# A sibling's front and first refills, and another order of the last expert weights, in a block with a mixture of 32 experts

## Reference

```python
h = rms_norm(x, norm1_gain);  proj = h @ w_in               # columns: q,k,v | q_i (512), k_i (64), w_i (8) | retention
out_a = dsa_attention(...)    # each query attends to its 64 best keys by an indexer score
out_b = silu(g_b) * retention(...)
x = x + concat(out_a, out_b) @ w_out
h2 = rms_norm(x, norm2_gain)
logits = h2 @ w_router + b_router;  top 4 of 32, softmax over the four -> combine
for e in range(32):
    z = h2 @ w1[e] + b1[e]                                  # w1[e]: 1024 x 2048, 8 MiB
    act = clamped_swiglu(z)
    out += combine[:, e] * (act @ w2[e] + b2[e])            # w2[e]: 1024 x 1024, 4 MiB
x = rms_norm(x + out, final_gain)
```

## Time and profile before

| | |
|---|---|
| median of 3 runs | 1087.22 us (1087.14 to 1087.7) |
| the profiled execution | 1086.36 us |
| its span, first to last instruction | 1084.6 us |
| PE busy, share of the span | 1038.4 us, 96% |
| DVE, ACT, POOL busy | 302.7, 157.0, 22.2 us |
| DMA, mean over the span | 396 GB/s, 429.75 MB |
| mean granted clock of TensorE | 0.985 of 2.4 GHz |

### The profile page before, as it was taken

One profiled execution on the slowest core, in us unless ns is written; L12 is line 12 of the kernel. 1 busy time (PEld: TensorE's weight loads), 2 busy tenths in 40 slices (PEclk: granted clock), 3 DMA queues, 4 the chain that ended last, 5 costly groups with the idle time before them and its releaser, 6 DMA issues.

```text
span 1084.6 us, 11586 instructions
## 1 busy us (share of the span) xinstructions
PE 1038.4 (96%) x4616; PEld 397.4 (37%) x4616; DVE 302.7 (28%) x705; ACT 157.0 (14%) x281; POOL 22.2 (2%) x29
## 2 busy tenths in 40 slices
PE   9999999999999999899999999898989898999996
PEld 7458454333333333233332323232323232333332
DVE  2455623322222223122221312221223222221221
ACT  1231333110101111101010111011111101011111
POOL 1212000000000000000000000000000000000000
PEclk9999999999999999999998999999999999899999
DMA  9886946999999999999999999999999999999995
GB/s 328 238 252 264 387 161 242 429 431 432 432 426 431 433 430 429 431 433 429 429 431 433 428 430 432 425 432 430 431 433 431 433 431 428 430 433 431 424 428 208
DMA packets 34343, 429.75 MB, mean 396 GB/s; under 512 B 5036, under 2 KB 6480, under 8 KB 16496
## 3 DMA queue, kind: packets, MB, share of 16 engines
q1 hardware_dynamic: 32400, 426.03, 93.2%
q10 hardware_dynamic: 1216, 1.70, 1.1%
q0 software_dynamic: 704, 1.71, 0.6%
HBM read 426.80 MB, written 2.62 MB: 396 GB/s over the span
## 4 chain that ended last, share of the span: by engine, by line
PE 67%; DMA 31%; DVE 1%; SPq 1%; issue 0%; ACT 0%; DVEq 0%
PE ps L1326 28%; DMA w1r<-w_mlp 22%; PE ps L1352 13%; DMA w2r<-w_mlp 6%; PE ps L1393 5%; PE ps L1076 4%; PE ps L1304 3%; PE ps L1064 3%; DMA w1r<-w_out 1%; PE ps L1123 1%; PE ps L1229 1%; PE ps L1366 1%; PE ps L1198 1%; DMA w1r<-w_in 1%; PE ps L1334 1%; PE ps L1312 1%
## 5 line engine op out<-in xcount | busy, mean ns | idle before, releaser
L1326 PE MATMUL ps<-w1r,arena 128*64 128x512 f32 x2048 | 487.7, 612 | 28.0 <-DMA w1r<-w_mlp 27.2
L1326 PEld LDWEIGHTS ps<-w1r,arena 128*64 128x64 f32 x2048 | 139.2, 139 | 295.7 <-issue 257.5
L1352 PE MATMUL ps<-w2r,arena 128*64 128x512 f32 x960 | 211.8, 593 | 4.5 <-DMA w2r<-w_mlp 4.5
L1352 PEld LDWEIGHTS ps<-w2r,arena 128*64 128x64 f32 x960 | 68.7, 137 | 142.8 <-issue 135.3
L950 DVE TENSOR_TENSOR acc<-ps,acc 128x512 f32<-128x512 f32 x56 | 36.1, 686 | 180.5 <-PE ps L1393 180.5
L942 DVE TENSOR_TENSOR arena<-arena 128x512 f32<-128x512 f32 x32 | 22.2, 692 | 157.5 <-ACT arena L571 157.4
L575 ACT ACTIVATE arena<-ps 128x512 f32<-128x512 f32 x32 | 19.1, 597 | 289.0 <-PE ps L1334 289.0
L914 DVE TENSOR_TENSOR arena<-ps,cols 128x512 f32<-128x512 f32 x32 | 22.1, 692 | 137.6 <-PE ps L1312 135.9
L1304 PE MATMUL ps<-h,arena 128*64 128x512 f32 x248 | 58.5, 592 | 0.0
L1393 PE MATMUL ps<-arena 128*128 128x512 f32 x112 | 55.5, 618 | 0.0
L580 ACT ACTIVATE arena<-ps 64x512 f32<-64x512 f32 x29 | 17.1, 591 | 263.8 <-PE ps L1352 263.8
(11 more groups left out here) (252 smaller groups left out, 575.4 us busy)
## 6 DMA issues: line engine op xcount, KB each, us to landing
w1r<-w_mlp SPq DMA_DIRECT2D x54, 4096.0 KB, 32.0
w2r<-w_mlp SPq DMA_DIRECT2D x60, 2048.0 KB, 18.9
w1r<-w_mlp SPq DMA_DIRECT2D x22, 2048.0 KB, 10.6
w1r<-w_in SPq DMA_DIRECT2D x7, 2048.0 KB, 17.3
w1r<-w_out SPq DMA_DIRECT2D x2, 2048.0 KB, 13.7
w1r<-w_mlp SPq DMA_DIRECT2D x3, 1024.0 KB, 7.3
rel_table<-arena ACTq DMA_DIRECT2D x1, 1536.0 KB
acc<-x SPq DMA_DIRECT2D x2, 512.0 KB, 4.6
```

The costliest lines, as they stand in the source:

```text
L1326: ins = mm(ps[64 * c:64 * c + 64, 2 * par + n, :], hgT[:, par, k % 4, 64 * (k // 4):64 * (k // 4) + 64], w1r[:, 8 * par + k, at:at + 512], ...
L1352: ins = mm(ps[at:at + 64, 4 + c, :], actT[:, k % 4, 64 * (k // 4):64 * (k // 4) + 64], w2r[:, k // 2, col:col + 512], start=(k == 0), stop ...
```

## The change

At the start: the three gain rows are loaded by SP's queue, not ACT's; the 72 columns and the 512 columns (now 584 together, `qiw` in `w1r` rows 12 to 15) come in two transfers over four of the eight row blocks each; PE does the keys' products of both token tiles for the first half, then for the second, then the relative table's product and the query columns.

Router to first expert: the slot numbers carry the offset `FAR`, so that `place` doesn't subtract it. The product of `ones` for the second tile comes before the first gather, the bias products of expert 0 after the second ranking product. The first gather's copy, transposes and scaling are done in two halves (`take_first_hgT`), and the first weight rows wait for the first half alone.

First steps: in expert 0's step the gather for expert 1 moves from behind row 1 to behind row 6, its transposes from row 3 to row 7; in expert 1's step to rows 3 and 4. Refills: rows 0 to 3 of expert 2 and rows 0 and 1 of expert 3 are loaded singly (`by_row`), the rest in pairs.

At the end: experts 28 to 31 are loaded in pairs instead of halves (31 was already); second weight 29 goes ahead of first weight 31; second weight 30 goes into `w2r` behind it, so that `down` serves it; 31 goes into `w1r` rows 0 to 3. `final` is put in another order accordingly: the transposes of expert 30's activation and the sum of the last full pair move up, `down` of expert 30 is split around the opening of the second sum. The result is stored by two transfers of 512 KB, where there were four of 256 KB. One counter (`pair_count`) replaces the laps.

The diff, cut to what the prediction speaks of; semaphore declarations, ACT's counterpart of `final` and the later sweeps are left out:

```diff
         mixT = carve(arena, 0, [KD, S])
-        wki = carve(arena, 0, [KD, 72])
+        qiw = carve(high, 0, [KD, 584])
         relT, onehot, relb = carve(arena, 576, [REL]), carve(arena, 1088, [REL]), carve(arena, 1600, [AH])
         L = carve(arena, 2048, [AH, KW])
         bsrc = carve(arena, 2048, [2048])
...
             sp.dma_start(acc[:, 1, :], x_v[:, 1]).then_inc(x_in[1], 16)
-            sp.dma_start(wki, win_v[:, :, 2048:2120]).then_inc(wki_in, 16)
-            load_win(0)
+            sp.dma_start(gain_rows[0:8, :], norm1_gain[0].rearrange("(k p) -> k p", p=P)).then_inc(gain_in, 16)
+            sp.dma_start(gain_rows[8:12, :], ret_gn_gain[0].rearrange("(k p) -> k p", p=P)).then_inc(gain_in, 16)
+            sp.dma_start(gain_rows[12:20, :], norm2_gain[0].rearrange("(k p) -> k p", p=P)).then_inc(gain_in, 16)
+            for i in range(2):
+                sp.dma_start(qiw[:, 4 * i:4 * i + 4], win_v[:, 4 * i:4 * i + 4, 1536:2120]).then_inc((wki_in, win_in[0])[i], 16)
             sp.dma_start(bsrc[0:32, :], b_mlp1[0]).then_inc(bias_in, 16)
             load_win(1)
...
-                for e, at in ((NE - 2, 0), (NE - 1, 4)):
-                    sp.wait_ge(w1_used, 8 * base + 8 * (NE - 2) + at + 2)
-                    sp.dma_start(w1r[:, at:at + 2, :].rearrange("p a f -> p (a f)"), w2_v[e, 0]).then_inc(w2_last[at // 2], 16)
-                    sp.wait_ge(w1_used, 8 * base + 8 * (NE - 2) + at + 4)
-                    if at == 0:
-                        sp.dma_start(w1r[:, 2:4, :].rearrange("p a f -> p (a f)"), w2_v[e, 1]).then_inc(w2_last[1], 16)
-                    else:
-                        sp.dma_start(w1r[:, 6, :], w2_v[e, 1, :, 0:2048]).then_inc(w2_last[3], 16)
-                        sp.dma_start(w1r[:, 7, 0:1024], w2_v[e, 1, :, 2048:3072]).then_inc(w2_last[4], 16)
-                        sp.dma_start(w1r[:, 7, 1024:2048], w2_v[e, 1, :, 3072:4096]).then_inc(w2_last[5], 16)
+                e, done = NE - 1, 8 * base + 8 * (NE - 2)
+                sp.wait_ge(w1_used, done + 2)
+                sp.dma_start(w1r[:, 0:2, :].rearrange("p a f -> p (a f)"), w2_v[e, 0]).then_inc(w2_last[0], 16)
+                sp.wait_ge(w1_used, done + 4)
+                sp.dma_start(w1r[:, 2, :], w2_v[e, 1, :, 0:2048]).then_inc(w2_last[1], 16)
+                sp.dma_start(w1r[:, 3, 0:1024], w2_v[e, 1, :, 2048:3072]).then_inc(w2_last[2], 16)
+                sp.dma_start(w1r[:, 3, 1024:2048], w2_v[e, 1, :, 3072:4096]).then_inc(w2_last[3], 16)
             def rest_of_sweep(base):
...
-                sp.wait_ge(w1_used, 8 * base + 1)
-                sp.dma_start(w1r[:, 0, :], w1_v[2, 0, 0, :, 0:2048]).then_inc(w1_early, 16)
-                sp.wait_ge(w1_used, 8 * base + 2)
-                sp.dma_start(w1r[:, 1, :], w1_v[2, 0, 0, :, 2048:4096]).then_inc(w1_in[0], 16)
-                next_w1(base, 2, 0, range(1, 4))
-                next_w1(base, 3, 1)
+                def by_row(e, par, rows):
+                    for k in rows:
+                        sp.wait_ge(w1_used, 8 * base + 8 * (e - 2) + k + 1)
+                        sp.dma_start(w1r[:, 8 * par + k, :], w1_v[e, k // 4, k // 2 % 2, :, 2048 * (k % 2):2048 * (k % 2) + 2048]).then_inc(w1_in[4 * par + k // 2], 16)
+                by_row(2, 0, range(4))
+                next_w1(base, 2, 0, range(2, 4))
+                by_row(3, 1, range(2))
+                next_w1(base, 3, 1, range(1, 4))
                 ahead(1, 4, 0)
                 ahead(2, 5, 1)
...
                     between(2 * m - 1, 2 * m + 1, 1)
                     between(2 * m, 2 * m + 2, 0)
-                with sp.Fori(6, NE // 2 - 1) as m:
+                with sp.Fori(6, 13) as m:
                     ahead(2 * m - 1, 2 * m + 1, 1)
                     ahead(2 * m, 2 * m + 2, 0)
+                ahead(25, 27, 1)
+                for e in range(26, 29):
+                    next_w2(base, e)
+                    next_w1(base, e + 2, e % 2)
+                next_w2(base, NE - 3)
                 next_w1(base, NE - 1, 1)
-                next_w2(base, NE - 3)
+                next_w2(base, NE - 2)
                 last_w2(base)
...
+            sp.dma_start(fgb, final_gain.rearrange("(a d) -> a d", a=1).to_broadcast((P, D))).then_inc(last_dma, 16)
             out_v = out[0].rearrange("(t p) d -> p t d", p=P)
-            for i, (t, c) in enumerate(((0, 0), (0, 1), (1, 0))):
-                sp.wait_ge(res_ready, i + 1)
-                sp.dma_start(out_v[:, t, 512 * c:512 * c + 512], res[:, t, 512 * c:512 * c + 512]).then_inc(stored, 16)
+            sp.wait_ge(res_ready, 2)
+            sp.dma_start(out_v[:, 0], res[:, 0, :]).then_inc(last_dma, 16)
             sp.wait_ge(fin_root, 3)
-            sp.dma_start(out_v[:, 1, 512:1024], res[:, 1, 512:1024]).then_inc(stored, 16)
-            sp.wait_ge(stored, 64)
+            sp.wait_ge(res_ready, 3)
+            sp.dma_start(out_v[:, 1], res[:, 1, :]).then_inc(last_dma, 16)
+            sp.wait_ge(last_dma, 48)
...
                 dve.wait_ge(mm_done, count)
                 link(v.scalar_tensor_tensor(rank[:, t, :], ps[:, 6, 64 + NE * t:64 + NE * t + NE], FAR, chosen[:, t, :], ALU.add, ALU.mult))
-                link(v.tensor_scalar(rank[:, t, :], rank[:, t, :], -FAR, None, ALU.add))
                 v.tensor_scalar(onehotP[:, 0, t, :], slotn, rank[:, t, 0:1], st[:, 6 + t:7 + t],
                                 ALU.is_equal, ALU.mult).then_inc(first_pick, 1)
...
@@ -915,6 +920,16 @@
                                 cols[:, GQ:GQ + 8].rearrange("p (b a) -> p b a", a=1).to_broadcast((P, 8, SLOTS)),
                                 ALU.mult).then_inc(hgT_sb, 1)
+            def take_first_hgT():
+                for i in range(2):
+                    dve.wait_ge((first_made, hg_tr)[i], 2 - i)
+                    ins = v.tensor_tensor(hgT[:, 0, 2 * i:2 * i + 2].rearrange("p j (c n) -> p (j c) n", c=2),
+                                          ps[:, 7 - i, 256 * i:256 * i + 256].rearrange("p (b n) -> p b n", b=4),
+                                          cols[:, GQ + 4 * i:GQ + 4 * i + 4].rearrange("p (b a) -> p b a", a=1).to_broadcast((P, 4, SLOTS)),
+                                          ALU.mult)
+                    ins.then_inc((hgT_part, hgT_sb)[i], 1)
             def gated_one_hot(base, hb, e, m, par, free=True):
...
                 ins.then_inc(proj_done, 1)
-            pe.wait_ge(wki_in, 16)
-            for t in range(TT):
-                pe.wait_ge(hT_ready, 2 * t + 2)
-                ins = one_tile(wki, 0, 72, t)
+            for i in range(2):
+                pe.wait_ge((wki_in, win_in[0])[i], 16)
+                for t in range(TT):
+                    pe.wait_ge(hT_ready, 2 * t + i + 1)
+                    for k in range(4 * i, 4 * i + 4):
+                        ins = mm(ps[:, t, 0:72], hT[:, k, P * t:P * t + P], qiw[:, k, 512:584], start=(k == 0), stop=(k == KD - 1))
             ins.then_inc(proj_done, 1)
             pe.wait_ge(rel_in, 32)
...
             pe.wait_ge(cols_sb, 1)
-            chunk(C_QI, 2, by_head)
+            by_head(qiw, 2).then_inc(proj_done, 1)
...
             x2_T(1, 1)
             route(1)
-            pe.wait_ge(bias_part, 3)
-            pe.wait_ge(sel_first, 1)
-            z_bias(0, 0, 0, free=False)
+            mm(ps[:, 6, 64 + NE:64 + 2 * NE], ones, chosen[:, 0, :], start=True, stop=False)
             gather_first(0)
-            mm(ps[:, 6, 64 + NE:64 + 2 * NE], ones, chosen[:, 0, :], start=True, stop=False)
             pe.wait_ge(chosen_ready, 2)
             mm(ps[:, 6, 64 + NE:64 + 2 * NE], before, chosen[:, 1, :], start=False, stop=True).then_inc(rank_mm, 1)
+            pe.wait_ge(bias_part, 3)
+            pe.wait_ge(late_consts, 2)
+            z_bias(0, 0, 0, free=False)
             gather_first(1).then_inc(first_made, 1)
             mm(ps[:, 5, 0:NE], ones, chosen[:, 0, :], start=True, stop=False)
             mm(ps[:, 5, 0:NE], ones, chosen[:, 1, :], start=False, stop=True).then_inc(count_mm, 1)
-            pe.wait_ge(first_copied, 1)
-            for j in range(4):
-                ins = nc.tensor.transpose(ps[:, 7, P * j:P * j + P], hg[:, P * j:P * j + P], ident)
-            ins.then_inc(hg_tr, 1)
+            for i in range(2):
+                pe.wait_ge(first_copied, i + 1)
+                for j in (2 * i, 2 * i + 1):
+                    ins = nc.tensor.transpose(ps[:, 7 - i, P * j:P * j + P], hg[:, P * j:P * j + P], ident)
+                ins.then_inc((first_made, hg_tr)[i], 1)
...
...
-            def step(base, hb, wb, rb, m, par, first=False, last=False):
+            def step(base, hb, wb, rb, m, par, first=False):
...
+                start = head and isinstance(base, int)
+                gather_at, turn_at = (6, 7) if head else (3, 4) if first else (1, 3)
+                pe.wait_ge(hgT_part if start else hgT_sb, 1 if start else base + e + 1)
+                if not start:
                     z_bias(base, e, par, free=not first)
```

(76 more changed lines are left out.)

97 lines of the change are left out of this document (44 added, 53 removed).

## The result

| | before | after |
|---|---|---|
| median | 1087.7 us (1087.14 to 1091.59, 5 runs) | 1094.46 us (1092.91 to 1096.01, 5 runs) |
| span of the profiled execution | 1084.6 us | 1092.6 us |
| mean granted clock, of 2.4 GHz | 0.985 | 0.978 |
| PE busy | 1038.4 us | 1044.1 us |

The changed kernel is slower, by a ratio of 1.0055, with a 95% interval of [1.004, 1.007]. The prediction was 1085.2, and its range ended at 1087.6.

What follows compares the result with a forecast made beforehand. PE was taken to bound 173 to 432 us, DMA 432 to 1000 us. Stream -1.7 and end -0.3, with stores at 0, summed to -2.0, or 1085.2 us; range 1082.9 to 1087.6.

Steps and rivals of the forecast that it cites:

- step 1: Input projection: key and small products wait for the second half-load, query columns start 2.2 us later (1.2 to 2.8).
- rival (c): Experts 28 to 31: waits drop the clock to 1.2 GHz; one fall behind weight 30 adds 2.4, giving 1087.6; chance 0.06.
- Step 2: Router to first expert: shorter ranking, moved products and a halved gather bring the first row 1.3 us sooner (1.0 to 1.6).
- Step 3: First refills: weight stream ends 1.7 us earlier (0.5 to 3.0), limited by the second half for expert 5.
- the late turning: Expert 0 to expert 1: transposes of expert 1 come after expert 0's last row, costing PE 0.5 us.
- my gapless stream: First refills: weights could flow without gaps from 179.1, ending at 1065.2 or 1066.1, the latter 2.8 us before today.
- step 4: Kernel end: last group starts 5.9 after the last landing, 0.3 us sooner (-0.8 to +0.4); the stream stays whole.
- Step 5: Result stores: two of 512 KB replace four of 256 KB; taken as 0, bounded by 0.6 us either way.
- the late ends of my other bounds: Slow limits: input projection +2.8, router to first expert -1.0, kernel end +0.4, result stores +0.6 us.
- Rival (b): First refills: four more rows loaded singly each lose 1.8 us, giving 1091.3; chance 0.05.
- Rival (d): Whole kernel: the change does nothing, as the front takes what the restart gives, 1087.2; chance 0.10.

Runs made afterwards that it cites:

- warmer_start: Changed kernel with 4 and 5 products of zeros on PE ahead of the waits for the two column loads; 1091.6 us, ratio 1.0037.
- old_start: Changed kernel with the loads and PE order of the kernel before put back at the input projection; 1087.09 us, ratio 0.9995.
- new_start_only: Kernel before with the changed start and nothing else; 1094.58 us, ratio 1.0062.
- lead_less_a: Kernel before with 7 extra products on PE ahead of the rows of expert 3; 1086.51 us, one run.
- lead_less_b: Kernel before with 14 extra products on PE ahead of the rows of expert 3; 1089.27 us, one run.
- warm_start: Changed kernel with 1 and 2 products of zeros on PE ahead of the waits for the two column loads; 1092.01 us, ratio 1.0039.
- all_pairs: Changed kernel with the old start, experts 2 and 3 refilled by pairs of rows only; 1088.26 us, one run.
- best: Changed kernel with old start, two products of zeros before the query columns, halves for experts 4 and 5 split, four stores; 1086.13 us, ratio 0.9983.
- split_halves: Changed kernel with the old start, first half for expert 4 and second for expert 5 each issued as two pairs; 1087.03 us, ratio 0.999.

## Why the prediction was wrong, step by step

The forecast of the difference was -2.0, and the spans show +8.0. The 10.0 between them come from the steps as follows. The step that failed above all is step 1: its term for the products behind the new waits.

**Step 1, the input projection: +2.2 forecast, +7.2 measured, 5.0 of the error.** The order was read rightly: half of the key products and the small one stand behind the second half of the load. Two terms failed. The second half was taken to land at 13.8; it landed at 14.6, no sooner than the whole load before (14.35). That is 0.8, and 0.2 beyond the late end of my bound. The other 4.2 is the clock: 1.8 on the second 16 products, 0.6 on the small product and its transpose, 1.8 on the query columns. I costed the products by their full-speed duration (1.9, 1.0, and 14.05 for the query columns as before), though the same step gives PE two waits that it didn't have. They took 3.7, 1.6 and 15.9. A third term was put at nothing, the gain loads in SP's queue: behind them the two column loads are issued at 2.7 and 3.2, where they were issued at 1.7 and 2.1. How much of the 0.8 that is was not tried. I had rows that show the price of such a wait, and used them for the end of the kernel alone, as rival (c) with 0.06. At the start it was the case that came: of the five kernels with the new start, the clock fell in four, in all but warmer_start. That the delay would reach the end undiminished was right, as the earlier trace rows say: the first weight row of after comes 6.0 later, with 1.2 of gain between.

**Step 2, router to first expert: -1.3 forecast, -1.2 measured.** From the start of the query columns to the first row it was 159.4 before and is 158.2 in old_start. Right, by its own terms.

**Step 3, the first refills: the stream was to end 2.6 sooner relative to the first row, and ended 1.1 later in the profile, 3.7 of the error.** The 0.5 for the late turning was right (0.4 measured). The 3.7 have three parts.

The first 1.45: I took the second half for expert 5 as the limit and let it come 2.6 sooner, but the transfer ahead of it was only 1.15 sooner relative to the first row (94.85 against 96.0). The first refills of after do land sooner, by 1.7 at the last pair for expert 2 (25.0 against 26.7), not by the 3.7 of my gapless stream, and some of the 1.7 is lost again before expert 5.

The next 0.85 is the lead. I took 2.4 as the time that a transfer needs ahead of its bytes, from a refill of 1 MiB on an idle queue, and applied it to one of 4 MiB in a running stream, which came late in most executions with 4.0 or less. Its lead fell from 5.5 to 4.0, as the stream was 1.15 ahead and PE 0.35 behind relative to the first row.

The last 1.4 lie behind that half, where step 4 says that the stream stays whole. From its landing to that of the last weights it is 789.2 to 789.7 in the four profiles with the old order (before, new_start_only, lead_less_a, lead_less_b) and 790.6 to 791.8 in all eight others, for the same bytes. In six of the eight a transfer soon after that half came 0.4 to 1.0 late, and in five one or two of the last ones 0.7 to 1.4, though they were issued over 20 us ahead; in the four others none came more than 0.3 late. So this is no lack of lead, and it goes with the new order. Its cause stays open.

Over the five profiles with these refills and whole halves, the last weights land 894.8 (warm_start), 895.6, 896.0, 896.1 and 897.0 (warmer_start) after the first row. So the stream gains nothing, and whether it loses half a microsecond or more stays open.

**Step 4, the end: -0.3 forecast, 0.0 measured.** The second half of second weight 30 lands 9.9 before the last weights, as forecast. PE's work behind it is 15.9 (15.8 forecast), and 0.1 passes from landing to first product, which I had left out; the rest is rounding. No clock fall there: rival (c) did not come where I had put it.

**Step 5, the stores: 0 forecast, +0.9 in the profile.** My bound of 0.6 was too tight. The six profiles with two stores take 10.45 to 11.0 from the last group to the end, four of the six with four stores 9.5 to 9.6 and two 10.1 and 10.4, so the form costs about 0.9 in most executions. The last store then carries twice the bytes and lands 1.2 later after its issue (4.7 against 3.5), of which its issue 0.3 sooner gives little back.

Rival (b) is refuted by all_pairs: its stream ends no sooner without the short rows. The Trainium skill's figure for a transfer of 1 MB ("DMA: Bandwidth & Descriptors", section Bandwidth), which I had weighed there, is from a table of transfers issued by GpSimd, where SP issues these, and the traces don't bear it out: the later single rows of old_start landed 2.5 apart, near the stream's rate, the first two 3.2 and 2.8. Rival (d) gives the time of old_start: without the new start the change does nothing that can be measured. Its mechanism, a front that takes what the restart gives, is not what happened: in the changed kernel the front alone costs 6.0, and the restart gives nothing. A range that took the clock's price on step 1 (+4.2), no gain in step 3, and the late ends of my other bounds (+2.8, -1.0, +0.4, +0.6) as one case would have reached 1094.

## What to carry to other kernels

Where a change gives TensorE a new wait, look first at what it did in the microseconds around it and at the granted clock: the wait itself may be small beside the products behind it at half speed, and in a PE-bound stretch nothing gives that back. Work thrown away in such a wait is worth trying, as in warmer_start, but where the load is already in it only costs time, as in the profile of best. Look at several executions: the same start kept its clock in five profiles and lost it in two. A queue's lead has to be measured for the size of transfer that stands in it: take the tightest transfer, delay its issue on purpose, and read in more than one execution when it comes late.

## What the runs showed of the hardware

Waits of 1 to 2 us were enough to bring the clock down early in the kernel. In the changed kernel PE waited 1.60, worked 2.00, and the clock fell 0.9 into the next wait. In new_start_only the stretch from 10 to 15 already has 0.64 after a wait of 1.84. With the old start the clock fell in two of seven profiles, both with a wait of over 1.2 for the gain rows; a wait of 1.11 later on left it at 1.00 (split_halves).

The second half for expert 5, a transfer of 4 MiB, came late in five of six profiles with leads of 2.9 to 4.0 us and in none of four with 4.1 to 5.5, though a 1 MiB one on an idle queue had needed 2.4 ahead of its bytes. The Trainium skill ("DMA: Bandwidth & Descriptors", section Anatomy of one DMA) gives, for transfers that GpSimd issues, a fixed cost of about 2.0 us that doesn't grow with size. SP issued these; the 2.4 is near that figure, the lead of about 4.0 is not, and why the larger transfer needs more lead was not tried.

The last store of the result landed 3.5 to 4.3 us after its issue where it carried 256 KB (six profiles), and 4.7 to 5.3 where it carried 512 KB (six profiles).
